# Expert loop of a hybrid decoder step: routing and loop in one block, gathered rows turned on VectorE, down halves copied out on ScalarE

## The reference, cut to what matters

```python
scores = sigmoid(t @ w_router)                       # 264 x 64 experts
# 4 of 8 expert groups, then the best 6 experts of each token
w = scores[chosen] / sum(scores[chosen]) * 2.5
routed = sum over the 6 chosen e:  w[t,e] * ((silu(t @ w_gate_e[e]) * (t @ w_up_e[e])) @ w_down_e[e])
shared = (silu(t @ w_gate_s) * (t @ w_up_s)) @ w_down_s
x = x + g2 * rms_norm(routed + shared)
```

## Time and profile before

| | |
|---|---|
| time, median of 3 runs | 930.7 us (930.54 to 934.95) |
| profiled execution, span | 935.2 us |
| PE busy | 876.3 us (94%) |
| VectorE busy | 329.2 us (35%) |
| ScalarE busy | 199.0 us (21%) |
| POOL busy | 155.1 us (17%) |
| DMA | 325.47 MB, mean 348 GB/s |

### The profile page before, as it was taken

How to read it: one execution, slowest core, us unless ns; L and a number is a source line. 1 busy time by engine, 2 the same in 40 slices (tenths; PEclk the granted TensorE clock), 3 DMA queues, 4 the chain that set the end, 5 groups by cost and what they waited for, 6 DMA issues and landing times.

```text
span 935.2 us, 18109 instructions
## 1 busy us (share of the span) xinstructions
PE 876.3 (94%) x7475; PEld 564.8 (60%) x7475; DVE 329.2 (35%) x795; ACT 199.0 (21%) x507; POOL 155.1 (17%) x185
## 2 busy tenths in 40 slices
PE   5899999997899899999899999999999999989987
PEld 3788888875666668756755555554555555444442
DVE  2315580047334598536322322222121221222214
ACT  2000110316222299024011111111111111101012
POOL 0000000022467000000312121121212212212110
PEclk9999999999899999999999999999999999999998
DMA  9966766737499947999999999999999999999993
GB/s 370 379 230 242 286 261 238 301 97 256 148 290 345 377 168 260 419 417 403 351 413 412 416 424 418 420 417 424 419 422 415 426 416 422 419 422 419 421 404 137
DMA packets 61237, 325.47 MB, mean 348 GB/s; under 512 B 16321, under 2 KB 25394, under 8 KB 40610
## 3 DMA queue, kind: packets, MB, share of 16 engines
q1 hardware_dynamic: 47218, 305.53, 81.4%
q0 software_dynamic: 12176, 18.56, 5.9%
q10 hardware_dynamic: 1760, 0.20, 0.2%
HBM read 326.65 MB, written 15.81 MB: 366 GB/s over the span
## 4 chain that ended last, share of the span: by engine, by line
PE 36%; DMA 13%; DVE 1%; SPq 0%; issue 0%; ACT 0%
PE bank L2428 19%; DMA slot_b<-in_w_e 13%; PE bank L2368 9%; PE bank L2379 4%; PE bank L2344 3%; PE bank L2438 1%; PE bank L2414 1%; SPq L1699 0%; DVE slot_b L2750 0%; DVE slot_b L2758 0%; PE bank L2398 0%; PE bank L2406 0%; ACT slot_b L2579 0%; DVE ht L2660 0%; DVE con L2652 0%
## 5 line engine op out<-in xcount | busy, mean ns | idle before, releaser
L420 PE MATMUL bank<-h,ring 128*128 128x264 f32 x608 | 138.4, 388 | 0.5 <-PE bank L420 0.3
L420 PEld LDWEIGHTS bank<-h,ring 128*128 128x128 f32 x608 | 114.6, 190 | 21.9 <-issue 2.6
L2652 DVE TENSOR_TENSOR con<-scales_of,bank 64x256 f32<-64x256 f32 x64 | 27.2, 425 | 270.5 <-ACT scales_of L2561 270.5
L1719 POOL DMA_INDIRECT xg<-tok_rows,tab_g x32 | 32.4, 1013 | 330.1 <-PE bank L2344 298.9
L2561 ACT ACTIVATE scales_of<-bank 64x256 f32<-64x256 f32 x64 | 24.2, 378 | 282.8 <-PE bank L2428 282.8
L2428 PE MATMUL bank<-done_out,xt 128*64 128x256 f32 x704 | 78.8, 381 | 3.7 <-DMA done_out<-in_w_e 2.8
L2428 PE MATMUL bank<-ring,xt 128*64 128x256 f32 x672 | 78.2, 386 | 0.0
L2428 PEld LDWEIGHTS bank<-done_out,xt 128*64 128x64 f32 x704 | 50.3, 137 | 33.9 <-issue 5.7
L2428 PEld LDWEIGHTS bank<-ring,xt 128*64 128x64 f32 x672 | 46.9, 138 | 35.7 <-issue 11.8
L2379 PE MATMUL bank<-sq,con 64*128 64x512 f32 x256 | 65.6, 609 | 0.0
L2368 PE MATMUL bank<-ring,ht 128*32 128x512 f32 x288 | 65.3, 595 | 0.0
(11 more groups left out here) (493 smaller groups left out, 1326.0 us busy)
## 6 DMA issues: line engine op xcount, KB each, us to landing
ring<-in_w_units SPq DMA_DIRECT2D x25, 2048.0 KB, 11.4
done_out<-in_w_e SPq DMA_DIRECT2D x22, 2048.0 KB
ring<-in_w_e SPq DMA_DIRECT2D x20, 2048.0 KB
slot_b<-in_w_e SPq DMA_DIRECT2D x11, 2048.0 KB
slot_f<-in_w_e SPq DMA_DIRECT2D x10, 2048.0 KB
ring<-in_w_e SPq DMA_DIRECT2D x16, 1024.0 KB
slot_b<-in_w_e SPq DMA_DIRECT2D x9, 1024.0 KB
done_out<-in_w_e SPq DMA_DIRECT2D x9, 1024.0 KB
```

The lines of the kernel that those rows point to most:

```text
L420: mm = pe.matmul(bank[:, t % NB, 0:T], w[:, j, k, :], h[:, k, :], start=(k == 0), stop=(k == KD - 1))
L1719: pool.indirect_dma_start(xg[q % AHEAD][:, :], None, tok_rows, bass.IndirectOffsetOnAxis(ap=tab_g[:, q:q + 1].bitcast(U32), axis=0), bound ...
L2652: dve.tensor_tensor(hh[e % 2][:, :], sg[e % 2][:, :], bank[LB:2 * LB, 4 + e % 2, 0:FE], ALU.mult).then_inc(hh_ready, 1)
```

## The change

Both blocks become one: routing and loop run without a common end between them. Buffers are laid out anew for that, `xt` becomes two buffers, and `slot_f` loses its down part, so that down weights have 6 buffers and expert 6's go to `w_sd`, over the rows `h2`. Lists hold at most 28 tokens (`LS`). The other 4 places of each 32 hold the eight sample tokens in every pair (4 in the upper, 4 in the lower block of 64): their rows are put into both `xg` once, by eight small DMAs, and gathers leave them alone. Their outputs aren't scattered; VectorE adds them up with their weights in `acc` (`add_own`), and the read-back of `choice_rows` is gone. The key of a list entry loses the rank, one table column operation and the four masked copies of the lists go, and PE's order of the shared parts and table matmuls changes. In the loop, turning moves from PE to VectorE, and `half_out` from VectorE to ScalarE. The core of the diff:

```diff
-SLOTS, DSLOTS = 6, 7
+OWN = 4
+LS = HB - OWN
+SLOTS, DSLOTS = 6, 6
 ...
             def gather(pool, q):
                 if q >= AHEAD:
-                    pool.wait_ge(xt_done, 2 * (q - AHEAD) + 2)
+                    pool.wait_ge(xt_ready, 2 * (q - AHEAD) + 2)
 ...
 SP
-                        load_dn(sp, 6)
                         for n, j in enumerate(SGU_ORDER):
 ...
+                        sp.wait_ge(fresh, 1)
+                        sp.dma_start(comb[:, :], io["comb"]).then_inc(comb_in, 16)
+                        sp.dma_start(same_row, io["same_row"]).then_inc(comb_in, 16)
+                        load_dn(sp, 5)
+                        sp.wait_ge(rows_stored, 32)
+                        sp.dma_start(w_sd[:, :, :]..., io["w_e"][EXTRA][:, GU:EW]).then_inc(w_sd_in, 16)
 ...
-                                for n in (e + 4, e + 5):
+                                for n in (e + 3, e + 4):
 ...
-                        sp.wait_ge(scattered, 1)
-                        sp.dma_start(cr_s, choice_rows[TP * TOPK:T * TOPK, :]).then_inc(read_back, 16)
 POOL
-                        pool.dma_start(tok_rows[TP:T, :], rows_s[:, :]).then_inc(rows_stored, 16)
+                        for i in range(AHEAD):
+                            for x4 in range(4):
+                                pool.dma_start(xg[i][x4 * HB + LS:(x4 + 1) * HB, :], rows_s[x4 % 2 * OWN:x4 % 2 * OWN + OWN, :]).then_inc(own_in, 16)
+                        pool.wait_ge(own_in, 16 * 4 * AHEAD)
+                        pool.wait_ge(rows_stored, 32)
                         pool.wait_ge(tab_ready, 1)
+                        for q in range(AHEAD):
+                            gather(pool, q)
 ...
-                            scatter_samples(q - 2)
 PE
-                            if q + 1 < NPAIR:
-                                for h in range(2):
-                                    turn_half(q + 1, h)
                             turn_inner(q)
 ACT
+                        def half_out(n):
+                            q, h = n // 2, n % 2
+                            act.wait_ge(half_done, n + 1)
+                            if q >= NYO:
+                                act.wait_ge(comb_done, 2 * (q - NYO) + h + 1)
+                                act.wait_ge(acc_ready, q - 1)
+                            act.copy(yo[q % NYO][:, h * 512:(h + 1) * 512], bank[:, 6 + h, :]).then_inc(y_ready, 1)
+                        for e in range(NE):
+                            act.wait_ge(gu_done, e + 1)
+                            ...
+                            act.activation(sg[e % 2][:, :], bank[0:LB, 4 + e % 2, 0:FE], ACT.Silu).then_inc(sg_ready, 1)
+                            if e % 2 and e >= 2:
+                                half_out(e - 3)
+                                half_out(e - 2)
+                        half_out(NE - 2)
+                        half_out(NE - 1)
                         act.activation(spare2[:, :], eps, ACT.Sqrt)
 DVE
+                        def turn_rows(q, h):
+                            if h == 0:
+                                dve.wait_ge(x_in[q % AHEAD], 16 * (q // AHEAD + 1))
+                            if q >= 2:
+                                dve.wait_ge(gu_done, 2 * q - 3 + h)
+                            for l in range(2):
+                                at = slice(h * LB + l * HB, h * LB + (l + 1) * HB)
+                                rows = xg[q % AHEAD][at, :].rearrange("p (k r c) -> p r k c", k=KD, r=4)
+                                for r in range(4):
+                                    ins = dve.transpose(xt[q % 2][32 * r:32 * r + 32, :, at], rows[:, r, :, :])
+                            ins.then_inc(xt_ready, 1)
+                        def add_own(q):
+                            dve.wait_ge(y_ready, 2 * q + 2)
+                            ...
+                                ins = dve.scalar_tensor_tensor(acc[:, :], yo[q % NYO], own_w[:, q:q + 1], acc[:, :], ALU.mult, ALU.add)
                         for q in range(NPAIR):
                             for e in (2 * q, 2 * q + 1):
+                                if q + 1 < NPAIR:
+                                    turn_rows(q + 1, e % 2)
                                 dve.wait_ge(sg_ready, e + 1)
                                 ...
                             if q:
                                 weight_matrix(q - 1)
-                                half_out(2 * q - 2)
-                                half_out(2 * q - 1)
                             ...
+                            if q:
+                                add_own(q - 1)
```

More of the change, by code:

```diff
@@ L115 @@
                   ("valid", NT), ("later", NBLK - NE),
[L116 removed]
+                  ("count", MAXOVER), ("same_head", NH), ("code", NT), ("second", 1)):
     CONSTS[_name] = (_at, _at + _n)
@@ L1770, in _, with overflow @@
+                                        bounds_check=TP - 1, oob_is_err=False).then_inc(x_in[q % AHEAD], 16)
+            def overflow(eng):
+                eng.wait_ge(over_ready, 1)
+                return eng.value_load(over[0:1, 0:1], min_val=0, max_val=MAXOVER)
+            with nc.Block() as block:
                     @block.sync
@@ new lines, in _ @@
+                        gather(pool, AHEAD)
+                        pool.wait_ge(tab_stored, 32)
+                        gather_weights(0)
+                        gather_weights(1)
+                        gather(pool, AHEAD + 1)
+                        for q in range(2, NPAIR):
+                            if q + AHEAD < NPAIR:
+                                gather(pool, q + AHEAD)
+                            gather_weights(q)
+                            if q == NPAIR // 2:
+                                more = overflow(pool)
@@ L1900, in _ @@
                         shared(0, 0, 0, P)
-                        pe.matmul(bank[NE:2 * NE, 5, 256 + P:256 + P + TS], ident[0:TS, NE:2 * NE], ident[0:TS, 0:TS], start=True, stop=True)
-                        pe.wait_ge(key_ready, 2)
+                        shared(0, 0, P, T - P, low)
+                        pe.wait_ge(key_ready, 1)
                         pe.transpose(bank[0:NE, 5, 256:256 + P], key[:, 0, :], ident)
-                        pe.transpose(bank[0:NE, 5, 256 + P:256 + P + TS], key[0:TS, 1, :], ident[0:TS, 0:TS])
@@ new lines, in combine @@
+                        def combine(n):
+                            q, h = n // 2, n % 2
+                            pe.wait_ge(y_ready, n + 1)
+                            pe.wait_ge(w_ready, q + 1)
+                            for l in range(2):
+                                at = slice(l * LB, (l + 1) * LB)
+                                mm = pe.matmul(bank[:, 2 * l + h, :], wmat[q % 2][at, :], yo[q % NYO][at, h * 512:(h + 1) * 512],
+                                               start=(q == 0), stop=(q == NPAIR - 1))
+                            mm.then_inc(comb_done, 1)
@@ new lines, in turn_inner @@
+                        def turn_inner(q):
+                            pe.wait_ge(hh_ready, 2 * q + 2)
+                            for e in range(2):
+                                for k in range(2):
+                                    at = FE + (2 * e + k) * LB
+                                    mm = pe.transpose(bank[:, 4, at:at + LB], hh[e][:, k * P:(k + 1) * P], eye)
+                            mm.then_inc(ht_done, 1)
+                        pe.wait_ge(fresh, 1)
+                        for h in range(2):
+                            turn_rows(0, h)
@@ L1988, in _ @@
+                        act.wait_ge(sum_done, 1)
+                        square(4, slice(0, P), bank[:, 4, 0:QD], junk)
+                        act.wait_ge(sum_done, 2)
+                        act.activation(inv[:, 2:3], bank[:, 5, 0:1], ACT.Sqrt, bias=eps, scale=1.0 / D).then_inc(inv_rooted, 1)
+                        act.wait_ge(y_done, 3)
+                        for c in (2, 3):
+                            store(act, io["y"][TP:T, c * QD:(c + 1) * QD], y_s[32 * c:32 * c + TS, :])
                     @block.vector
```

1087 lines of the change are left out of this document (469 added, 618 removed).

## The result

The changed kernel takes 940.5 us (median of four runs, 938.4 to 940.8) beside 930.7 us for the kernel before, a ratio of 1.0085 with a 95% interval of 1.0067 to 1.0103. Two later comparisons of the same kernel gave 1.0074 (1.0046 to 1.0102) and 1.0097 (1.0065 to 1.0129). By these ratios the change makes the kernel slower by 7 to 9 us. The prediction, 927.8 us with a range of 924 to 936.5, was wrong in size and in sign.

What follows compares the result with a forecast made beforehand. DMAs at about 420 GB/s were taken to bound the kernel. Terms -1.0 - 0.5 - 0.9 - 2.0 + 1.0 = -3.4 us gave 927.3 on the median, stated as 927.8 us, range 924 to 936.5.

Steps and rivals of the forecast that it cites:

- The start of the loop: Between routing and first gate_up: own rows land at 449, first buffer free at 462.8, DMA idle 0.2 instead of 2.2 us: -2.0.
- Rival A: Loop start: the eight own-row DMAs land one after another, delaying the first gather; +7.2 instead of -2.0, 936.5 us; chance 0.13.
- the transposes: VectorE in the loop: 16 transposes a pair at 0.43 us each, 6.9 us, within 9.8 us of work in 15.5.
- PE's 31.6 us: Loop: turning leaves PE, 1.02 us a pair over 31 pairs, nearly all of it covered by the DMAs.
- rival C: Loop: the DMAs weren't the limit, so PE's 1.02 us would count in each pair, giving 899 us; chance 0.05.
- rival B: Loop: VectorE becomes the bound if a transpose takes over 0.79 us; 960 us at 0.85, +105 us at 1.0; chance 0.09.
- rival D: First pairs of the loop: fewer down buffers starve PE, at most a few us, 933 us; chance 0.08.
- Last turning off PE: Pair 31: one turning behind the last awaited load leaves PE, -1.0 us, or 0 if the last down loads catch it.
- Order of down loads: Loop: down loads follow in the order PE needs them, between 0 and -1.2 us, taken as -0.5.
- Sample bytes: Loop: sample rows no longer gathered and scattered, 0.39 MB less on saturated DMAs, -0.9 us.
- Table load: Tail: ScalarE's table load now stands behind the last two `half_out`, delaying the squares, +1.0 us (bounds 0 and +1.1).

## Why the prediction was wrong

**The step that failed** is the start of the loop, "The start of the loop ... -2.0". I bounded the last own row's landing by 442.4 + 8.6 = 451.0, the flight of the single small DMA in the earlier trace rows, and took 449. In time from the mark: first issue forecast at +47.6, measured at +48.0; last issue forecast at +51.6, measured at +51.6; landing forecast at +58.2 with an upper bound of +60.2, measured at +63.4. The issues were right, the flight of the last was not: 11.8 us, 37% above the bound. The eight flights say why (issue to landing, L1914):

```profile
DMA to landing us min/median/max: 7.9/9.6/11.8
```

The first one took 7.9 us, within the bound, and the last 11.8. They were issued 0.51 us apart and, from 441.6 to 449.0, landed 1.06 us apart on average. The sum took the last of eight as if it flew alone, and left out that it stands behind seven others. A flight measured once, for one DMA behind the store of `h2`, isn't an upper bound for eight sent in a row.

**What hung on it.** The last own row landed 5.2 us later than forecast, and the first buffer came free 7.5 us later. The gather landed in 7.9 us (7.3 expected); the first turning began at +72.2 (forecast 457 - 390.85 = +66.2). I had PE idle 2 us; it was 8.4, and the clock of 0.50 stretched the first gate_up to 5.33 us, above my 4.8. The first buffer was free at +79.5, forecast +72.0, upper bound +76.7.

**Rival A was what happened**, own rows landing one after another, and I gave it 0.13 at 936.5. Its turning point, own rows after 452 (+61.2), was passed. Its sizes were others: it had them 1.5 us apart from 447.1 on, the last at +66.8 and the first buffer free at +81.2, later than measured. And yet it was priced too low. With the measured +79.5 its rule gives (79.5 - 71.8) - 2.2 = +5.5 us, and the bytes show +7.6. Of these 6.1 lie from +72 to +84 and 1.2 ahead of +56, which no term of mine had. The low rates from 448 to 452 (264 and 190 GB/s) aren't a part of it: from +56 to +72 the kernel before moved 317 GB/s and the changed one 301, which is 0.6 us.

**Right:** the transposes (0.43 us taken, 0.436 measured, 496 of them); that the DMAs set the pace (420 GB/s, 1.01); that PE's 31.6 us are hidden (rival C is out: PE was busy 26 us less and nothing was gained); that VectorE is not the bound at 16 transposes a pair (rival B), though its reach was put too far; six down buffers cost nothing that can be told (rival D, shown on the kernel before). The section "Rules for kernel authors" of the Trainium skill, VectorE: DVE Perf Modes, leaves 128x128 transposes to TensorE. The runs don't contradict it and confirm it only in part: with PE turning the time is 4.4 +- 3.6 us lower beside late own rows, and 0.7 +- 2.4 us lower with the early start, which is no difference that can be told.

**Other terms.** Last turning off PE, -1.0: 0 in the trace of the changed kernel, since PE waits for gate weights at the last expert there anyway (the chain ends its last wait for a load at 914.36). Order of down loads, -0.5: can't be told from 0. Sample bytes, -0.9: too small to be seen singly. Table load, +1.0: +0.8. No drain stood beside the 1.28 us of the load here either, so the 1.38 us of the Trainium skill, ScalarE: Activation LUTs, section "What ACT_TABLE_LOAD costs", aren't borne out by this trace.

**The range.** Half the chance should have gone to the start. The text named one queue, full DMAs and eight transfers that must land before anything else moves, and then took the middle of a bound made from one flight.

## What to carry to other kernels

Small transfers on the way to the first piece of a loop cost the flight that they have beside the loads, here 9.5 to 13.1 us for the last of eight, and the engine that they kept idle started at half its clock; place such data with an engine that is free, or take it out of the first piece. When a loop is bound by loads, count the bytes moved in the stretch ahead of it: here that number told the end better than any engine's busy time. And an upper bound taken from one row is an estimate.

## What the runs showed of the hardware

Eight DMAs of 16 KB from SBUF to SBUF, issued 0.5 us apart from POOL's queue while weights moved, took 11.2 to 12.7 us for the last one in the eight traces with this code, and 13.1 in the kernel before with the wait added; issued 0.6 us apart from ScalarE's queue it was 9.5. PE's granted clock at the first turnings was 0.50 in all ten of these traces, after 4.8 to 10.8 us of idle, and eight turnings then took 1.94 us in place of 1.06. In the kernel before they took 1.60 us after 3.02 us of idle, and in the one with six down buffers 1.07 after 1.87. After 1.55 us of idle at pair 0 the clock fell to 0.50 in the three traces with own rows by PE and VectorE turning, and stayed at 1.00 in the changed kernel and with own rows left out; what makes the difference isn't shown. With the square root moved ahead, ScalarE loaded a table behind the branch that wasn't taken and another before the next Sqrt; in the changed kernel one load served the squares and the roots of the tail.
